# Two of twelve stores of gate blocks issued two chunks later in the ScalarE program of a PEER block kernel

## The chip, the cores and the metric

The kernel runs on one core of one Trainium2 chip. The metric is the device time of one execution in microseconds. The kernel before took 1569.04 us (median of 3 runs, 1568.71 to 1569.89).

## The reference

One transformer layer on 512 tokens of width 1024, in fp32: an adaptive RMS norm, a mixer with three kinds of attention heads, and then a PEER feed-forward, to which this change belongs. Cut to the feed-forward:

```
q = (x @ wq) as 8 heads x 2 halves x 128
s = q . sub_keys                     # 128 keys for each half
sv, si = top_k(s, 16)                # for both halves
top, pos = top_k(sv[0] + sv[1], 16)  # 16 experts of 16384 for each head
eidx = 128 * si[0][pos] + si[1][pos]
g = softmax(top)
a = gelu(u[eidx] . x)
y = sum(g * a * v[eidx])
```

A token uses 128 of 16384 experts. u and v are tables of 16384 rows of 1024.

## The kernel before, in words

The tokens are four tiles of 128. For the first tile (GT = 1) the rows of u and v of the chosen experts are gathered one by one, late in the kernel. The other three tiles (DT = 384 tokens) are computed densely: the experts are cut into 128 chunks of 128 (chunk i has the first key i in the order of `u_t`), each chunk's a = gelu(u x) is made for all 384 tokens, multiplied by a dense matrix of gates that is zero where an expert was not chosen, and then multiplied by v.

**A chunk of u.** SyncE loads 512 KB into one of two places of `u_raw` (`load_u`, L1080), once u_lo of the chunk two before has been made. ScalarE rounds it to `u_hi` (`u_high`, L1435; it also waits until TensorE is through with the chunk two before). VectorE subtracts to get `u_lo` (`split_u`, L2003). TensorE runs 24 matmuls of 128x128 by 384 columns (L857 to L859: hi by hi, hi by lo, lo by hi, for 8 parts of the width), into one of two PSUM banks. ScalarE takes the gelu of it into `a_act` (`gelu`, L1472) and, for the first 56 chunks, stores the 192 KB to `spill` in DRAM (`early_gelu`, L1484). In ScalarE's program `u_high(i + 2)` stands ahead of `early_gelu(i)`.

**The gates.** For each of the three dense tiles VectorE decodes the experts' two key numbers (`decode`, L2010 to L2025), TensorE turns them to columns (L872), and VectorE copies these to `cols` (L2051). Then, for 4 tokens at a time, VectorE makes one-hot rows `hot_i` and `hot_j` (L2058, L2060), TensorE multiplies them (L886), and ScalarE copies the result to `g_out` (L1506). A block is 32 tokens: eight such steps, 2 MB in `g_out`, which has two places. At the end of a block ScalarE waits for its own copies and issues the store of the block to `gates` in DRAM (L1512, L1513). There are 12 blocks, `tb` from 0 to 11, four in each tile.

**The order.** It is written out by hand. Beside each block run two chunks of u, chunk `beside(tb)` and the one after. Between the tiles come chunks without gates, `BETWEEN`: chunks 0 to 23 ahead of the first tile of gates, 32 to 35 between the first and the second, 44 to 51 between the second and the third, 60 to 63 behind the third. So block 3 (chunks 30 and 31) is followed by chunk 32 and block 7 (chunks 42 and 43) by chunk 44. VectorE's program has the decoding of the next tile among the chunks between, and `split_u` of the chunk that follows them (36 after the first tile) ahead of the copy to `cols`:

```
for n in rest + [BETWEEN[tile].stop]:
    split_u(n)
ps = taken(dve, ("cols", tile))
dve.tensor_copy(cols[:, :, tile * P:tile * P + P], ...)
```

TensorE's program has the transposes to columns in the middle of the last chunk between the tiles (35 and 51), and each gates matmul ahead of a quarter of a chunk.

The stores of the gates and of the gelus are issued on ScalarE's DMA queue, the loads of u on SyncE's. Both use the same 16 DMA engines. The semaphores `s_gst` count the gate stores of either place of `g_out`; ScalarE waits for them before it fills the place again, and SyncE and VectorE wait for all of them before the second half of the work begins.

Of the kernel before, what the change touches and what calls it, by code (L numbers as in the profile page):

```python
# [9 lines left out]
NT = S // P  # L10
# [8 lines left out]
GT = 1  # L19
DT = S - GT * P  # L20
GB = 32
# [76 lines left out]
def peer_block_kernel(nc, x, c_col, norm1_col, w_ada, b_ada, w_in, w_out, lam_vecs, subln_row, sinks_row,  # L98
# [4 lines left out]
    with ctx:  # L103
# [3 lines left out]
        def sem(name):  # L107
            return ctx.enter_context(nc.semaphore(name))
# [4 lines left out]
        def at(name, kib, shape, dt=f32):  # L113
            return nc.alloc_sbuf_tensor_at(name, shape, dt, offset=base + int(kib * 1024))
# [73 lines left out]
        g_out = [at("g_out0", 112, [P, P, GB]), at("g_out1", 140, [P, P, GB])]  # L188
# [102 lines left out]
        s_hot, s_gm, s_gt = sem("hot_rows_ready"), sem("gates_made"), sem("gates_taken")  # L291
        s_as, s_al = [sem("gelus_stored0"), sem("gelus_stored1")], [sem("gelus_loaded0"), sem("gelus_loaded1")]
        s_gst = [sem("gates_stored0"), sem("gates_stored1")]
        s_x2, s_f2, s_fm, s_fs, s_res = (sem(n) for n in ("x2_ready", "x2_squares", "x2_mean", "x2_std", "result_ready"))

        gates = nc.dram_tensor("gates", [DT // GB, P, NCHUNK, GB], f32).ap()
# [7 lines left out]
        def after(eng, s, n):  # L304

            if isinstance(n, int) and n < 1:
                return
            eng.wait_ge(s, n)

        def within(i, last=NCHUNK - 1):  # L310

            return not isinstance(i, int) or i <= last
# [47 lines left out]
        def over(i, c, n):  # L360

            return i // n if isinstance(i, int) else (i - c) // n + c // n
# [3 lines left out]
        BETWEEN = [range(0, 24), range(32, 36), range(44, 52), range(60, 64)]  # L366
# [7 lines left out]
        def beside(tb):  # L374

            return BETWEEN[tb // 4].stop + 2 * (tb % 4)
# [65 lines left out]
        for J, (i, j) in enumerate(JOBS):  # L442
            for qt, kk, _, _ in plan[j][1]:
                for n in (TILES.index(qt), TILES.index(kk)):
                    if n not in known:
                        NEEDS[J] = NEEDS.get(J, []) + [n]
                        known.add(n)
            v = {"C": 3, "A": 7, "B": 12}[plan[j][0]]
            if v not in known:
                VALUES[J] = [v]  # L450
                known.add(v)
# [4 lines left out]
        def _(pe):  # L456
# [170 lines left out]
            def pv(J):  # L627


                i, j = JOBS[J]  # L630
                kind, _, _, _, col, _, n, _ = plan[j]
                g = GROUP_OF[J]
                b = f"O{g % 2}"
                ps = take(b, ("o", g)) if J == FIRST[g] else bank[b]
                for v in VALUES.get(J, ()):
                    for t in range(NT):
                        emptied(("v", v, t))
                emptied(("pT", J))
                ahead = kind == "B" and n >= 4
                first = col if ahead else col - HD  # L640
                place = HD + n * HD if ahead else n * HD
                kt = key_tiles(i, j)
                for a, t in enumerate(kt):
                    mm = pe.matmul(ps[:, place:place + 2 * HD], pT[:, J % 2, a * P:a * P + P],  # L644
                                   v_sb[:, t, first:first + 2 * HD], start=(a == 0), stop=(a == len(kt) - 1))
                mm.then_inc(full[b] if J == LAST[g] else s_pv, 1)
# [297 lines left out]
            def both(m, c, late, _):  # L944
                if at_end(m):
                    if m == NCHUNK - TAIL:
                        last_v_chunks()
                    return
                v_chunk(m, c)
                if not late and not (isinstance(m, int) and m + NEXT >= NCHUNK):  # L950
                    a_chunk(m + NEXT, c + 1)
# [286 lines left out]
        def _(act):  # L1238
# [131 lines left out]
            for J in range(-1, N):  # L1370
# [14 lines left out]
                if J in LAST[0:4]:  # L1385
                    i = LAST.index(J)
# [42 lines left out]
            def u_high(i, c):  # L1429

                if not within(i):
                    return
                after(act, s_a, i - 1)
                act.wait_ge(s_u[c % 2], 16 * (over(i, c, 2) + 1))
                act.activation(u_hi[c % 2][:, :], u_raw[:, c % 2, :], ACT.Copy).then_inc(s_uhi, 1)  # L1435
# [18 lines left out]
            def v_high(i, c):  # L1454
                if not within(i):
                    return
                end = at_end(i)
                if end:
                    act.wait_ge(s_acc, PH * TOPK)
                else:  # L1460
                    after(act, s_yv, i - 1)
                act.wait_ge(s_v[c % 4], 16 * (over(i, c, 4) + 1))
                act.activation(v_hi_end[:, i % TAIL, :] if end else v_hi[:, c % 2, :], v_raw[c % 4][:, :], ACT.Copy)\  # L1463
                   .then_inc(s_vhi, 1)

            def gelu(i, slot, c):

                if not within(i):
                    return
                early = isinstance(i, int) and i < EARLY  # L1470
                act.wait_ge(s_a, i + 1)
                act.activation(a_act[:, bass.ds(slot, 1), :].rearrange("p o t -> p (o t)"),  # L1472
                               bank[f"S{c % 2}" if early else f"O{c % 2}"][:, 0:DT], ACT.Gelu).then_inc(s_gelu, 1)

            def early_gelu(i):

                if i >= SPILL:
                    act.wait_ge(s_as[i % 2], 16 * (SPILL // 2))
                    gelu(i, i % AHEAD, i)
                    return  # L1480
                after(act, s_as[i % 2], 16 * (i // 2))
                gelu(i, i % AHEAD, i)
                act.wait_ge(s_gelu, i + 1)
                act.dma_start(spill[i], a_act[:, i % AHEAD, :]).then_inc(s_as[i % 2], 16)  # L1484

            u_high(1, 1)
            for i in BETWEEN[0]:
                u_high(i + 2, i + 2)
# [3 lines left out]
                if NUMBERS_AT <= i < NUMBERS_AT + NT:  # L1492
                    t = i - NUMBERS_AT
# [6 lines left out]
            for tile in range(NT - GT):  # L1500
                for tb in range(4 * tile, 4 * tile + 4):
                    i = beside(tb)
                    after(act, s_gst[tb % 2], 16 * (tb // 2))
                    for b in range(GB // 4):
                        act.wait_ge(s_gm, tb * (GB // 4) + b + 1)
                        act.activation(g_out[tb % 2][:, :, 4 * b:4 * b + 4].rearrange("p i t -> p t i"),  # L1506
                                       bank[f"T{b % 2}"][:, :].rearrange("p (t i) -> p t i", t=4), ACT.Copy)\
                           .then_inc(s_gt, 1)
                        if b == 3:
                            u_high(i + 2, i + 2)  # L1510
                            early_gelu(i)
                    act.wait_ge(s_gt, (tb + 1) * (GB // 4))  # L1512
                    act.dma_start(gates[tb].rearrange("p i t -> p (i t)"),  # L1513
                                  g_out[tb % 2][:, :, :].rearrange("p i t -> p (i t)")).then_inc(s_gst[tb % 2], 16)
                    u_high(i + 3, i + 3)
                    early_gelu(i + 1)
                for i in BETWEEN[tile + 1]:
                    u_high(i + 2, i + 2)
                    early_gelu(i)
                    if i == EARLY - 2:  # L1520

                        act.wait_ge(s_gst[0], 16 * (BLOCKS // 2))
                        v_high(0, 0)
# [710 lines left out]
```

## Time and profile before

| | |
|---|---|
| median of 3 runs | 1569.04 us |
| the profiled execution's own time | 1569.89 us |
| its span, first to last instruction | 1568.1 us |
| TensorE busy | 1528.9 us, 98% |
| TensorE weight loads | 1364.6 us, 87% |
| VectorE busy | 1338.0 us, 85% |
| ScalarE busy | 660.4 us, 42% |
| GpSimd busy | 487.9 us, 31% |
| mean granted TensorE clock | 0.995 |
| moved by DMA | 398.77 MB, 254 GB/s on average |

In the rows PE is TensorE, DVE is VectorE, ACT is ScalarE, SP is SyncE; a q behind a name (ACTq, SPq) is a DMA issue on that engine. A time at the start of a line is us from the start of the span. In square brackets stands the idle time of the engine ahead of the instruction, and what ended it. Busy times of 98% are an average over the whole kernel; the change lies between 573 and 669 us.

### The profile page before, as it was taken

The numbers are of one execution on the slowest core, as the hardware profiler recorded it, in microseconds if no ns is written. First come the engines' busy times: TensorE is split into PE (matmuls) and PEld (weight loads), VectorE is DVE, ScalarE is ACT, GpSimd is POOL, SyncE is SP. The second block draws the span as 40 slices with busy tenths as digits, with TensorE's granted clock in tenths as the row PEclk, the third lists the DMA queues.
The fourth block names the chain that finished last, engine by engine and source line by source line (L and its number), as shares of the span: only waits on it lengthen the run. The fifth ranks groups of instructions, "written<-read, shape, count | busy, mean of one in ns | idle before, by whom it ended". The sixth has DMA issues, their size and how long they took to land.

```text
span 1568.1 us, 24587 instructions
## 1 busy us (share of the span) xinstructions
PE 1528.9 (98%) x8275; PEld 1364.6 (87%) x8275; DVE 1338.0 (85%) x2877; ACT 660.4 (42%) x1143; POOL 487.9 (31%) x450
## 2 busy tenths in 40 slices
PE   4999999999999999999999999999999999999997
PEld 4877767888999999999999999999999998888886
DVE  5688765649999989899698898899999998999977
ACT  3444563233344766647433333333333432333232
POOL 1121300033450000020265445456566663223000
PEclk9999999999999999999999999999999999999999
DMA  9744310132355565676799999999999999999773
GB/s 368 267 163 159 148 68 1 55 95 82 107 180 170 198 229 196 229 239 268 280 398 333 345 347 338 348 336 371 372 373 378 366 343 356 376 351 352 241 240 107
DMA packets 160468, 398.77 MB, mean 254 GB/s; under 512 B 11754, under 2 KB 75370, under 8 KB 158706
## 3 DMA queue, kind: packets, MB, share of 16 engines
q1 hardware_dynamic: 112992, 227.06, 41.7%
q0 software_dynamic: 36864, 134.23, 23.0%
q10 hardware_dynamic: 10514, 36.30, 5.9%
q8 instruction: 47, 0.77, 0.2%
q14 instruction: 51, 0.41, 0.1%
HBM read 359.27 MB, written 38.27 MB: 254 GB/s over the span
## 4 chain that ended last, share of the span: by engine, by line
PE 81%; DVE 14%; DMA 2%; ACT 2%; issue 1%; ACTq 0%; DVEq 0%; SPq 0%
PE bank_S L908 16%; PE bank_T L908 11%; PE bank_O L859 6%; PE bank_O L857 6%; PE bank_O L858 6%; PE bank_T L886 5%; PE bank_G L908 5%; PE bank_S L857 3%; PE bank_S L858 3%; PE bank_S L859 3%; PE bank_O L644 2%; DVE mod_acc L1910 1%; PE bank_S L611 1%; DVE v_sb L1903 1%; DVE v_sb L1916 1%
## 5 line engine op out<-in xcount | busy, mean ns | idle before, releaser
L1463 ACT ACTIVATE v_hi<-v_raw 128x1024 fp32r<-128x1024 f32 x124 | 131.7, 1062 | 332.5 <-PE bank_G L908 332.5
L1435 ACT ACTIVATE u_hi<-u_raw 128x1024 fp32r<-128x1024 f32 x128 | 135.9, 1061 | 244.8 <-PE bank_O L859 139.8
L1214 POOL COPY stage<-eidx 128x1 uint32<-128x1 uint32 (+1 forms) x128 | 75.5, 590 | 462.2 <-DVE eidx L2031 208.5
L857 PE MATMUL bank_S<-h_hi,u_hi 128*128 128x384 f32 x512 | 180.0, 352 | 0.7 <-DVE u_lo L2003 0.7
L1218 POOL DMA_INDIRECT row<-in_peer_u,stage x128 | 148.1, 1157 | 103.7 <-POOL stage L1214 103.7
L859 PE MATMUL bank_O<-h_hi,u_lo 128*128 128x384 f32 x512 | 171.9, 336 | 0.0
L857 PE MATMUL bank_O<-h_hi,u_hi 128*128 128x384 f32 x512 | 171.7, 335 | 0.0
L859 PE MATMUL bank_S<-h_hi,u_lo 128*128 128x384 f32 x512 | 171.6, 335 | 0.0
L858 PE MATMUL bank_S<-h_lo,u_hi 128*128 128x384 f32 x512 | 171.5, 335 | 0.0
L858 PE MATMUL bank_O<-h_lo,u_hi 128*128 128x384 f32 x512 | 171.5, 335 | 0.0
L2099 DVE SCALAR_TENSOR_TENSOR y<-row,wgt,y 128x1024 f32<-128x1024 f32 x128 | 166.0, 1297 | 0.0
L2109 DVE TENSOR_TENSOR v_lo<-v_raw,v_hi 128x1024 fp32r<-128x1024 f32 x124 | 152.0, 1226 | 12.3 <-ACT v_hi L1463 0.8
L2122 DVE SCALAR_TENSOR_TENSOR junk<-row,h 128x1024 f32<-128x1024 f32 x128 | 156.0, 1218 | 0.0
L1218 POOL DMA_INDIRECT row<-in_peer_v,stage x128 | 142.2, 1111 | 41.9 <-issue 30.3
L908 PE MATMUL bank_S<-v_hi,w_lo 128*128 128x512 f32 x372 | 125.4, 391 | 0.0
L908 PE MATMUL bank_S<-v_lo,w_hi 128*128 128x512 f32 x372 | 125.3, 391 | 0.0
L908 PE MATMUL bank_S<-v_hi,w_hi 128*128 128x512 f32 x372 | 125.3, 391 | 0.0
L1506 ACT ACTIVATE g_out<-bank_T 128x512 f32<-128x512 f32 x96 | 104.7, 1122 | 46.6 <-PE bank_T L886 38.2
L2058 DVE TENSOR_SCALAR hot_i<-iota_k,cols 128x128 f32<-128x128 f32 x384 | 107.2, 347 | 1.0 <-PE bank_T L886 0.2
L886 PE MATMUL bank_T<-hot_i,hot_j 128*128 128x128 f32 x768 | 101.8, 275 | 1.3 <-DVE hot_j L2060 1.3
L886 PEld LDWEIGHTS bank_T<-hot_i,hot_j 128*128 128x128 f32 x768 | 97.6, 191 | 3.8 <-issue 2.1
L857 PEld LDWEIGHTS bank_S<-h_hi,u_hi 128*128 128x128 f32 x512 | 96.5, 189 | 2.1 <-issue 1.9
(374 smaller groups left out, 3649.6 us busy)
## 6 DMA issues: line engine op xcount, KB each, us to landing
u_raw<-in_u_t SPq DMA_DIRECT2D x128, 512.0 KB, 4.9
v_raw<-in_peer_v SPq DMA_DIRECT2D x128, 512.0 KB, 6.8
gates<-g_out ACTq DMA_DIRECT2D x12, 2048.0 KB, 6.8
g_in<-gates SPq DMA_DIRECT2D x32, 768.0 KB, 10.5
ada_late<-in_w_ada SPq DMA_DIRECT2D x8, 2048.0 KB, 8.5
spill<-a_act ACTq DMA_DIRECT2D x56, 192.0 KB, 2.3
a_act<-spill SPq DMA_DIRECT2D x14, 768.0 KB, 10.3
w_raw<-in_w_in SPq DMA_DIRECT2D x20, 512.0 KB, 4.0
```

Of the source, the lines that this page charges most:

```text
L857: pe.matmul(ps[:, 0:DT], u_hi[q][:, kk], h_hi[:, GT:NT, k, :], start=(k == 0), stop=False)
L858: pe.matmul(ps[:, 0:DT], u_hi[q][:, kk], h_lo[:, GT:NT, k, :], start=False, stop=False)
L859: mm = pe.matmul(ps[:, 0:DT], u_lo[q][:, kk], h_hi[:, GT:NT, k, :], start=False, stop=(k == KD - 1))
L886: mm = pe.matmul(ps[:, tok * P:tok * P + P], hot_j[:, b % 2, tok, :], hot_i[:, b % 2, tok, :], start=True, stop=True)
L908: mm = pe.matmul(y_bank[t][half][:, :], w[:, q, tt], v[:, q, half * 512:half * 512 + 512], start=(first and n == 0), stop=False)
L1218: pool.indirect_dma_start(rows[slot][:, :], None, table[:, :], bass.IndirectOffsetOnAxis(stage[:, place:place + 1], 0))\
L1435: act.activation(u_hi[c % 2][:, :], u_raw[:, c % 2, :], ACT.Copy).then_inc(s_uhi, 1)
L1463: act.activation(v_hi_end[:, i % TAIL, :] if end else v_hi[:, c % 2, :], v_raw[c % 4][:, :], ACT.Copy)\
L2058: dve.tensor_scalar(hot_i[:, B % 2, tok, :], iota_k[:, :], cols[:, 0, n:n + 1], cols[:, 2, n:n + 1], ALU.is_equal, ALU.mult)
L2099: dve.scalar_tensor_tensor(out=y0[:, :], in0=rows[2 * place + 1][:, :], scalar=wgt[:, q], in1=y0[:, :], op0=ALU.mult, op1=ALU.add).then_in ...
L2109: dve.tensor_tensor(lo[:, q, :], v_raw[c % 4][:, :], hi[:, q, :].bitcast(f32), ALU.subtract)\
L2122: dve.scalar_tensor_tensor(out=junk[:, :], in0=rows[2 * place][:, :], scalar=1.0, in1=h2[:, 0, :], op0=ALU.mult, op1=ALU.mult, accum_out=d ...
```

## The change

The store of a block becomes a helper, `store_gates`. For the last block of the first and of the second dense tile (blocks 3 and 7) it is not issued at the end of the block, but after `u_high(i + 3)`, `early_gelu(i + 1)` and the `u_high` and `early_gelu` of the first chunk between the tiles. The other ten stores stay where they are.

```
+            def store_gates(tb):
+                act.wait_ge(s_gt, (tb + 1) * (GB // 4))
+                act.dma_start(gates[tb].rearrange("p i t -> p (i t)"),
+                              g_out[tb % 2][:, :, :].rearrange("p i t -> p (i t)")).then_inc(s_gst[tb % 2], 16)
...
-                    act.wait_ge(s_gt, (tb + 1) * (GB // 4))
-                    act.dma_start(gates[tb].rearrange("p i t -> p (i t)"),
-                                  g_out[tb % 2][:, :, :].rearrange("p i t -> p (i t)")).then_inc(s_gst[tb % 2], 16)
+
+                    wait = tb % 4 == 3 and tile < NT - GT - 1
+                    if not wait:
+                        store_gates(tb)
                     u_high(i + 3, i + 3)
                     early_gelu(i + 1)
                 for i in BETWEEN[tile + 1]:
                     u_high(i + 2, i + 2)
                     early_gelu(i)
+                    if wait and i == BETWEEN[tile + 1].start:
+                        store_gates(tb)
```

## Rows read from the trace of the kernel before

**Rows 1.** Busy time of each engine from 500 to 760 us, granted clock, DMA share, GB/s

```profile
500.00:760.00 260.00, 258.29 (x1756) 255.17 (x1755) 235.53 (x568) 161.69 (x177) 10.95 (x9) 1.00 0.63 227
```

**Rows 2.** Waits of TensorE, 500 to 760: us in total, times, longest us

```profile
PE bank_T L886 <- DVE hot_j L2060: 1.3, 3, 0.5
PE bank_S L857 <- DVE u_lo L2003: 0.4, 1, 0.4
```

**Rows 3.** Waits of ScalarE, 500 to 760

```profile
ACT u_hi L1435 <- DMA u_raw<-in_u_t: 15.9, 4, 4.7
```

**Rows 4.** Timeline of ScalarE, second tile's last store (start, us, what)

```profile
653.12 0.34 ACTq L1513 DMA_DIRECT2D gates<-g_out  x1
653.56 1.06 ACT L1435 ACTIVATE u_hi<-u_raw 128x1024 fp32r<-128x1024 f32 x1 [0.48 <-ACT g_out L1506]
...
658.60 0.33 ACTq L1484 DMA_DIRECT2D spill<-a_act  x1
663.26 1.06 ACT L1435 ACTIVATE u_hi<-u_raw 128x1024 fp32r<-128x1024 f32 x1 [4.69 <-DMA u_raw<-in_u_t]
```

**Rows 5.** Line L1513 from 653 to 654: us to landing

```profile
DMA to landing us min/median/max: 6.9/6.9/6.9
```

**Rows 6.** Chain that ended last, 560 to 700: two u_raw loads (start, us)

```profile
576.10 6.53 DMA u_raw<-in_u_t
...
655.98 7.19 DMA u_raw<-in_u_t
```

**Rows 7.** Line L1080 from 650 to 651 (one load, at 650.9)

```profile
DMA to landing us min/median/max: 3.6/3.6/3.6
```

**Rows 8.** Timeline of VectorE, second tile

```profile
664.42 1.23 DVE L2003 TENSOR_TENSOR u_lo<-u_raw,u_hi 128x1024 fp32r<-128x1024 f32 x1 [2.50 <-ACT u_hi L1435]
```

**Rows 9.** Timeline of TensorE, second tile, end of chunk 46 and start of 47

```profile
664.91 0.33 PE L858 MATMUL bank_S<-h_lo,u_hi 128*128 128x384 f32 x1
665.08 0.34 PE L859 MATMUL bank_S<-h_hi,u_lo 128*128 128x384 f32 x1
665.79 0.41 PE L857 MATMUL bank_S<-h_hi,u_hi 128*128 128x384 f32 x1 [0.38 <-DVE u_lo L2003]
```

**Rows 10.** Timeline of ScalarE, first tile's last store

```profile
573.23 0.34 ACTq L1513 DMA_DIRECT2D gates<-g_out  x1
...
578.71 0.33 ACTq L1484 DMA_DIRECT2D spill<-a_act  x1
582.71 1.06 ACT L1435 ACTIVATE u_hi<-u_raw 128x1024 fp32r<-128x1024 f32 x1 [4.03 <-DMA u_raw<-in_u_t]
```

**Rows 11.** Timeline of VectorE, first tile, u_lo of chunk 36

```profile
586.93 1.23 DVE L2003 TENSOR_TENSOR u_lo<-u_raw,u_hi 128x1024 fp32r<-128x1024 f32 x1
```

**Rows 12.** Timeline of TensorE, first gates matmul of the second and third tile

```profile
590.53 1.13 PE L886 MATMUL bank_T<-hot_i,hot_j 128*128 128x128 f32 x8 [0.48 <-DVE hot_j L2060]
...
687.61 1.13 PE L886 MATMUL bank_T<-hot_i,hot_j 128*128 128x128 f32 x8 [0.39 <-DVE hot_j L2060]
```

**Rows 13.** Line L1080, windows 579 to 581 and 659 to 660: when issued

```profile
L1080 SPq DMA_DIRECT2D u_raw<-in_u_t x1: 328/328/328, 579.7 to 579.7; - x1
...
L1080 SPq DMA_DIRECT2D u_raw<-in_u_t x1: 328/328/328, 659.5 to 659.5; - x1
```

**Rows 14.** DMA queues (q1 SyncE, q10 ScalarE): windows 654:659, 660:662.2, 659:660

```profile
q10 hardware_dynamic: 127, 2.08, 104.5%
q1 hardware_dynamic: 6, 0.01, 0.4%
...
q1 hardware_dynamic: 134, 0.50, 71.2%
...
q10 hardware_dynamic: 102, 0.13, 64.3%
```

**Rows 15.** Line L1513 from 573 to 574: us to landing

```profile
DMA to landing us min/median/max: 7.8/7.8/7.8
```

**Rows 16.** Tile g_out, all 12 gate stores: us to landing

```profile
DMA to landing us min/median/max: 6.5/6.8/8.4
```

## The prediction, made before the kernel was run

> **What bounds the kernel now.** I read the busy times by stretch first. From 500 to 760 us, the stretch in which the gates are made and stored, TensorE is busy for 258.29 of 260 us, at a granted clock of 1.00, so 2.4 GHz [rows 1]. Next I read whom TensorE waits for in that stretch: four waits, together 1.7 us, three for hot_j at the start of each tile's gates and one of 0.4 for a u_lo [rows 2]. Nothing else can be gained there. ScalarE does wait for loads of u_raw, 15.9 us in four waits [rows 3], but ScalarE is not the bound; such a wait costs only what reaches TensorE.
>
> The timeline shows where it does. In the second tile the last store of gates is issued at 653.12 and takes 6.9 us to land [rows 4, 5]. The u_raw load issued at 655.98 takes 7.19 us, where one with free DMA engines takes 3.6 [rows 6, 7]. Its u_hi starts at 663.26, u_lo at 664.42, and TensorE, whose matmuls follow one another each 0.17 us, starts the next chunk at 665.79 instead of one step after 665.08, at 665.26 [rows 4, 8, 9]: 0.53 us lost. In the first tile the same load, issued at 576.10, takes 6.53 us [rows 6]; u_hi comes at 582.71 [rows 10], and TensorE has no gap there. What follows in that tile is tight all the same: u_lo of chunk 36 (586.93), then the copy to cols, hot_i, hot_j, and the first gates matmul at 590.53 after a gap of 0.48 [rows 11, 12]. The third tile has 0.39 at the same place with no store before it [rows 12], so at most 0.09 us of that gap is the store's.
>
> **The change, part by part.** Everything here is reckoned on the profiled execution: 1569.89 us, of which the span is 1568.1. That execution is 0.85 above the median of 1569.04; differences are added to the median. A measurement of this kernel tells about 0.2%, 3.1 us, from no change.
>
> *Nothing is added in work.* Two stores of 2 MB, of 12, are issued later by ScalarE; the bytes, the instruction (0.34 us) and its wait stay. Where the wait stood, u_hi can start some 0.4 us earlier (653.56 less 653.12) [rows 4], but the u_hi behind it still waits for TensorE, so this is worth nothing. At the new place the wait for the gate copies is long fulfilled. The 0.34 us of issue lies in ScalarE's idle time before the next u_hi (4.69 us idle there before) [rows 4]. The buffer of the moved store is filled again two blocks later, behind eight copies, a store and two chunks of the other buffer; the moved store has landed long before, so no copy waits for it.
>
> *Gain.* The load of 655.98 no longer has the store in front. With 3.6 us, even with 5, it lands by 661.0, before TensorE frees its u_hi (a chunk of 4.16 us before 665.26, so 661.1). The gap of 0.53 us in the second tile goes. The 0.09 of the first tile I do not count, since the same buffer chain is late there for the next reason.
>
> *Cost.* The store is now issued right behind the spill store of the second chunk: about 0.4 after 578.71, so 579.1, and 0.4 after 658.60, so 659.0 [rows 4, 10]. Half a microsecond later SyncE issues the next u_raw loads, at 579.7 and 659.5 [rows 13]; these times are set by u_lo of the chunk two earlier, which does not move. Call L the time that these loads take.
>
> How late may they be? Second tile: chunk 47 starts at 665.26 with its gap gone, and 24 matmuls at 0.173 (a step of 0.17 in the rows) end at 669.42 [rows 9]. From start of u_hi to the first matmul is 665.79 - 663.26 = 2.53, from landing to u_hi 0.09 (655.98 + 7.19 = 663.17). So it must land by 666.8: L up to 7.3 is free. First tile: what counts is not TensorE's own need of chunk 36, which comes after the gates matmul, but VectorE's order. u_lo of chunk 36 stands ahead of the cols copy, and the copy ahead of hot_j. From u_lo to the gates matmul is 590.53 - 586.93 = 3.60; from u_hi to u_lo 1.16, landing to u_hi 0.09. Landing later than 590.53 - 4.85 = 585.7 delays TensorE one for one: L up to 6.0 is free. So:
>
> shift = (L - 6.0, not below 0) + (L - 7.3, not below 0) - 0.53.
>
> TensorE has no other wait in this stretch, so a shift at either place stays to the end.
>
> *L itself.* From 654 to 659 the ScalarE queue moved 127 packets, 2.08 MB, while the SyncE queue moved 6, though a load was issued at 655.98; that queue's 134 packets came at 660 to 662.2 [rows 14]. A load issued during the store is moved after it. So I take that one issued 0.5 us after it is as well. Before, the two loads landed 9.4 (576.10 + 6.53 - 573.2) and 10.05 us after their store's issue. Between stood a spill store, whose 102 packets kept the 16 engines 64% busy for 1 us, so 0.64 us [rows 14]; it now goes ahead of the store. This leaves 8.8 and 9.4, less the lag of 0.6 and 0.5: 8.2 and 8.9, mean 8.55. Those two stores took 7.8 and 6.9, mean 7.35, against a median of 6.8 over all 12 [rows 5, 15, 16]; with the median it would be 8.0. I take 8.3, between. Then the first tile costs 2.3, the second 1.0, less 0.53: **+2.8 us**, 1571.8. Bounds for L behind the store: below, 7.0 (the shortest store, 6.5, less the lag of 0.5, and the 1.6 us by which the first tile's load landed after its store, less the spill's 0.64); above, 9.5 (the second tile's 10.05 less 0.5, with the spill's 0.64 not gone). These give +0.5 and +5.2.
>
> The Trainium skill, "DMA: Bandwidth & Descriptors", section "Anatomy of one DMA — SWDGE (gpsimd) path", fits a transfer of GpSimd's path as 2.0 us plus its bytes by 436 GB/s: by it an estimate of 8.0 us for store and load as one, so L of 7.5 and a shift of +1.2. For the store alone it gives 6.8, which the trace agrees with; for the load alone 3.2, against 3.6 in the row.
>
> **Rivals.**
> *A. The whole tail comes on top (slower).* Place: the same two loads. If L is 8.5 or more, the shift is over 3.1 us; with 9.5 it is 3.5 + 2.2 - 0.5 = +5.2, 1574.2. For it speaks that one of the two loads seen landed 10.05 after the store's issue, and that the spill store of the next chunk and the next load queue up as well. Against it: ordinary stores take 6.5 to 6.8. The point of decision lies only 0.2 above the L that I take.
> *B. The queues share the engines (not slower).* The load is issued while the store has hardly begun, and its packets might get in between. With equal bytes each the load waits for as much of the store as it has itself, 0.5 of 2 MB, a quarter of 127 packets in 5 us: 3.6 + 1.25 = 4.9. L is below 6.0, nothing is late, and the shift is -0.5: 1568.5. For it speaks that store and load start together, which the trace does not show for 2 MB; against it, the 3 us in which a waiting load moved nothing.
> Here the Trainium skill, same page, section "Queues, rings and completion order", says that each DMA engine goes round between its queues, packet by packet. By that rule rival B would be nearer; the trace does not agree for the load of 655.98.
> That the change does not do what it says is ruled out by the code: the condition holds for blocks 3 and 7 and the loop issues each of them once, at chunks 32 and 44.
>
> **How the numbers follow.** Queued behind with L from 7.0 to 8.5: 0.52, time 1571.8. Rival A: 0.37, from 1572.2 to 1574.2. Rival B: 0.11, 1568.5. Under B the gain is far within 0.2%; I still leave 0.03 of its chance for faster, for what I don't see. So faster 0.03, same 0.52 + 0.08 = 0.60, slower 0.37. The range reaches from L = 7.0 less the spread of the median, 1568.9, to L = 9.5 with some 0.2 on top, 1574.4 (the runs of the kernel before lie within 0.9 of the median); what is outside is most of rival B and the end of A. The likeliest case's own range is 1569.5 to 1572.2.
>
> **What would show it.** In the trace after, the load near 655.6 to 656 takes 5 us or less, and the matmul gap near 665.3 is gone. The loads near 579.7 and 659.5 take 8 us or more, with ScalarE's u_hi waiting for them until about 588 and 668. TensorE waits near 590 for hot_j, 2.8 us instead of 0.5, and near 669.4 for u_lo, 1.0 us. If those loads take under 6 us the reckoning is wrong at L; if they take 8 and the gaps do not come, it is wrong at the order on VectorE. If the time moves by more than 5 us either way, something outside this stretch has moved.

## The result, and the profile after

The changed kernel takes 1574.14 us (median of 9 runs, 1573.13 to 1575.07), the kernel before in the same runs 1569.89 (9 runs, 1568.30 to 1570.62): 4.25 us slower, ratio 1.003 with an interval of 1.0022 to 1.0038. Run again on another occasion it took 1573.85 (median of 8 runs) against 1569.38, 4.47 us slower, ratio 1.0025 (1.0015 to 1.0036). That lies inside the range of the prediction, but on the side of its rival A: clear of noise, and slower by more than 0.2%.

The span grew from 1568.1 to 1572.4 us, and all of it in the stretch of the change. First the waits of TensorE from 500 to 765 us (us in total, times, longest), which answer to [rows 2]:

```profile
PE bank_T L886 <- DVE hot_j L2068: 3.5, 3, 2.7
PE bank_S L857 <- DVE u_lo L2011: 1.3, 1, 1.3
```

Before it was 1.3 and 0.4, so 3.1 us more of waiting. The timeline of TensorE has the two gaps, at the first gates matmul of the second tile [rows 12] and ahead of chunk 48:

```profile
592.35 1.13 PE L886 MATMUL bank_T<-hot_i,hot_j 128*128 128x128 f32 x8 [2.68 <-DVE hot_j L2068]
...
674.22 0.41 PE L857 MATMUL bank_S<-h_hi,u_hi 128*128 128x384 f32 x1 [1.26 <-DVE u_lo L2011]
```

Where they come from is on ScalarE's timeline, to be read beside [rows 4] and [rows 10]:

```profile
578.35 0.33 ACTq L1484 DMA_DIRECT2D spill<-a_act  x1
578.72 0.45 ACTq L1488 DMA_DIRECT2D gates<-g_out  x1
581.04 1.06 ACT L1435 ACTIVATE u_hi<-u_raw 128x1024 fp32r<-128x1024 f32 x1 [2.72 <-PE bank_S L859]
...
587.60 1.06 ACT L1435 ACTIVATE u_hi<-u_raw 128x1024 fp32r<-128x1024 f32 x1 [5.12 <-DMA u_raw<-in_u_t]
...
662.35 0.44 ACTq L1488 DMA_DIRECT2D gates<-g_out  x1
664.67 1.06 ACT L1435 ACTIVATE u_hi<-u_raw 128x1024 fp32r<-128x1024 f32 x1 [2.72 <-PE bank_S L859]
...
671.68 1.06 ACT L1435 ACTIVATE u_hi<-u_raw 128x1024 fp32r<-128x1024 f32 x1 [5.57 <-DMA u_raw<-in_u_t]
```

The chunk that waited for its load before (35 and 47) now waits for TensorE alone, at 581.04 and 664.67. The one behind it (36 and 48) waits for its load for over 5 us. The chain that ended last names both loads (start, us):

```profile
579.30 8.22 DMA u_raw<-in_u_t
...
662.93 8.67 DMA u_raw<-in_u_t
```

On VectorE the first of them holds up a queue of work, as the order in the code says (u_lo, cols, hot_i, hot_j):

```profile
588.77 1.22 DVE L2011 TENSOR_TENSOR u_lo<-u_raw,u_hi 128x1024 fp32r<-128x1024 f32 x1 [3.53 <-ACT u_hi L1435]
589.91 0.55 DVE L2059 COPY cols<-bank_G 128x384 f32<-128x384 f32 x1
590.49 1.11 DVE L2066 TENSOR_SCALAR hot_i<-iota_k,cols 128x128 f32<-128x128 f32 x4
591.52 0.68 DVE L2068 TENSOR_TENSOR hot_j<-iota_k,cols 128x512 f32<-128x512 f32 x1
```

The waits explain 3.1 of some 4.5 us. The rest is in no wait. It is in how long the matmuls take behind the first gap:

```profile
593.50 0.33 PE L858 MATMUL bank_S<-h_lo,u_hi 128*128 128x384 f32 x1
...
594.24 0.53 PE L858 MATMUL bank_S<-h_lo,u_hi 128*128 128x384 f32 x1
594.56 0.53 PE L859 MATMUL bank_S<-h_hi,u_lo 128*128 128x384 f32 x1
```

Their starts are 0.32 us apart instead of 0.17. The windows (stretch, its length, busy us and instructions of PE, PEld, DVE, ACT, POOL, then granted clock, DMA share, GB/s) show why:

```profile
592.30:593.70 1.40, 1.35 (x11) 1.38 (x12) 1.40 (x5) 0.12 (x1) 0.00 (x0) 1.00 0.87 336
593.70:597.10 3.40, 3.40 (x15) 3.40 (x14) 2.03 (x8) 1.25 (x2) 0.00 (x0) 0.50 0.01 4
597.10:600.50 3.40, 3.40 (x27) 3.40 (x26) 3.40 (x10) 1.96 (x2) 0.00 (x0) 0.99 0.00 0
```

For 3.4 us the granted clock is 0.50, 1.2 GHz, and TensorE gets through 15 matmuls instead of 27. The kernel before has 27 there at 1.00:

```profile
593.70:597.10 3.40, 3.40 (x27) 3.40 (x26) 3.40 (x9) 2.21 (x2) 0.00 (x0) 1.00 0.02 5
```

The engine is busy 3.40 of 3.40 us either way, so busy time does not show this loss. Before the clock fell, TensorE had waited 2.68 us, up to 592.35, and had then run for 1.35 us at 1.00.

So that the parts can be told apart, here are the starts of three instructions in each profiled execution: the transposes to columns at the end of the first stretch between tiles (A), the first gates matmul of the second tile (B), the transposes of the third tile (C).

| kernel | A | B | C | B - A | C - B | A to C against before |
|---|---|---|---|---|---|---|
| before | 587.47 | 590.53 | 684.62 | 3.06 | 94.09 | |
| changed | 587.09 | 592.35 | 688.86 | 5.26 | 96.51 | +4.62 |
| changed, again | 587.46 | 592.65 | 689.14 | 5.19 | 96.49 | +4.53 |
| block 3 alone | 587.38 | 592.64 | 686.07 | 5.26 | 93.43 | +1.54 |
| block 7 alone | 587.48 | 590.54 | 685.49 | 3.06 | 94.95 | +0.86 |
| u_lo behind hot rows | 587.52 | 590.57 | 686.50 | 3.05 | 95.93 | +1.83 |
| matmuls in the gap | 587.48 | 592.77 | 687.68 | 5.29 | 94.91 | +3.05 |
| block 3 alone, matmuls in the gap | 587.57 | 592.86 | 686.28 | 5.29 | 93.42 | +1.56 |
| store with the load | 586.26 | 591.02 | 686.85 | 4.76 | 95.83 | +3.44 |
| copy without a wait | 586.72 | 591.04 | 684.93 | 4.32 | 93.89 | +1.06 |
| store 1.1 us behind the load | 587.36 | 590.35 | 684.48 | 2.99 | 94.13 | -0.03 |
| two halves | 585.61 | 588.59 | 682.02 | 2.98 | 93.43 | -0.74 |

### The profile page after: what moved, and what is told of

Same layout as the page of the kernel before. It is cut to its first block, busy times and chain, and to the rows that moved or that the text cites. A ratio compares the mean times of both kernels' runs of the same rounds, so it can differ in the third digit from the quotient of the medians.

```text
span 1572.4 us, 24587 instructions
## 1 busy us (share of the span) xinstructions
PE 1529.5 (97%) x8275; PEld 1365.8 (87%) x8275; DVE 1337.3 (85%) x2877; ACT 659.6 (42%) x1143; POOL 485.3 (31%) x450
## 4 chain that ended last, share of the span: by engine, by line
PE 81%; DVE 14%; DMA 2%; ACT 1%; issue 1%; DVEq 0%; SPq 0%; ACTq 0%
PE bank_S L908 16%; PE bank_T L908 11%; PE bank_O L859 6%; PE bank_O L857 6%; PE bank_O L858 6%; PE bank_T L886 5%; PE bank_G L908 5%; PE bank_S L857 3%; PE bank_S L858 3%; PE bank_S L859 3%; PE bank_O L644 2%; DVE mod_acc L1918 1%; PE bank_S L611 1%; DVE v_sb L1911 1%; DVE v_sb L1924 1%
```

## The experiments

The theory after the result: (1) a load of u_raw issued half a microsecond behind a 2 MB store is moved after it and takes over 8 us; (2) in the first tile this reaches TensorE through VectorE's order, 2.2 us; (3) in the second, 1.4 us, less the gap removed; (4) TensorE's clock falls behind the longer gap, 1.4 us. The rivals stand with each run. Each difference is against the median of the kernel before in the same set of runs, and the ratio stands with its 95% interval.

**Block 3 alone.**

```
-                    wait = tb % 4 == 3 and tile < NT - GT - 1
+                    wait = tb == 3
```

> Only block 3 is stored two chunks on; block 7 is back at its old place. Theory (two late loads plus TensorE's clock): against the kernel before, +2.2 us for hot_j in the first tile, +1.4 us for the 3.4 us at half clock behind that gap, nothing in the second tile, where the gap of 0.5 at the end of chunk 46 stays: +3.6 us. Rival (the moved stores cost the same at both places, about half each): +2.1 us.

Measured: 1572.11 against 1569.40, +2.7 us (ratio 1.0016, 1.0007 to 1.0025). The gap is there in full:

```profile
592.64 1.13 PE L886 MATMUL bank_T<-hot_i,hot_j 128*128 128x128 f32 x8 [2.69 <-DVE hot_j L2068]
```

but the clock did not fall in this execution; the window of it reads

```profile
593.70:597.10 3.40, 3.40 (x26) 3.40 (x25) 3.40 (x11) 2.22 (x2) 0.00 (x0) 1.00 0.05 18
```

This was a miss in two ways. The first is the clock. The profiled execution, 1571.36 us, is the fastest of the 11, which go up to 1573.49, so it is not typical of them. Only the mean granted clock over the whole execution is on record for the others. A stretch of 3.4 us at half clock takes 0.001 from that mean (3.4 x 0.5 / 1570). It is 0.994 in 8 of the 11 and at least 0.995 in the three fastest, while 5 of the 33 executions of the kernel before beside them have 0.994 or less. So the clock most likely fell in most executions here; the measure is rough, since it also holds every other stretch at half clock. The second miss is C - B, 93.43, which is 0.66 below the kernel before with block 7 in its old place: the old gap of 0.53, most of that difference, is not in every execution either. The load behind that store took 6.5 us here, 7.19 in [rows 6].

**Block 7 alone.**

```
+                    wait = tb == 7
```

> Only block 7 is stored two chunks on. Theory: the load behind it takes 8.7 us, 1.4 more than is free, less the 0.53 gained at chunk 47: +0.9 us against the kernel before, with a gap of 1.3 us ahead of chunk 48 and the granted clock at 1.00 throughout. Rival (half of the loss each): +2.1 us.

Measured: 1570.80 against 1569.40, +1.4 us (ratio 1.0007, 0.9998 to 1.0016). The median and its interval could not tell 0.9 from 2.1, the trace does: +0.86 from A to C, the load 8.69 us, the gap 1.28, and the clock at 1.00.

```profile
659.55 8.69 DMA u_raw<-in_u_t
...
670.86 0.41 PE L857 MATMUL bank_S<-h_hi,u_hi 128*128 128x384 f32 x1 [1.28 <-DVE u_lo L2011]
```

**VectorE's order.** The change, with u_lo of chunk 36 made later:

```
-                for n in rest + [BETWEEN[tile].stop]:
+                for n in rest + ([BETWEEN[tile].stop] if tile != 1 else []):
                     split_u(n)
...
                                       ALU.is_equal).then_inc(s_hot, 1)
+                    if tile == 1 and B == tile * P // 4:
+                        split_u(BETWEEN[tile].stop)
```

> The changed kernel, but VectorE makes u_lo of chunk 36 behind the first hot rows of the second tile's gates instead of ahead of the copy to cols. Theory (VectorE's order carries the late load to TensorE): the load still takes 8.2 us, but the wait for hot_j falls from 2.7 to about 0.5 us, some 0.6 us return at the next two steps, and the clock stays at 1.00; the second tile's +0.9 stays: +1.4 us against the kernel before. Rival (chunk 36 itself is late on TensorE, or the loss lies elsewhere): +4.3 us as in the changed kernel.

Measured: 1571.05 against 1569.40, +1.65 us (ratio 1.0009, 0.9999 to 1.0018). ScalarE still waits 5.11 us for the load, but TensorE doesn't:

```profile
588.02 1.06 ACT L1435 ACTIVATE u_hi<-u_raw 128x1024 fp32r<-128x1024 f32 x1 [5.11 <-DMA u_raw<-in_u_t]
```

```profile
590.57 1.13 PE L886 MATMUL bank_T<-hot_i,hot_j 128*128 128x128 f32 x8 [0.47 <-DVE hot_j L2068]
593.34 1.13 PE L886 MATMUL bank_T<-hot_i,hot_j 128*128 128x128 f32 x8 [0.32 <-DVE hot_j L2068]
```

The gap at the first gates matmul is as short as in the kernel before, with a load just as late, and the clock stays at 1.00 (593.7 to 597.1). This shows (2): what was late for TensorE was not chunk 36 itself but the columns' copy behind its u_lo. The new order has a price of its own: the fifth gates matmul starts at 599.36, against 598.37 with block 7 alone. That is nearly all of the 0.98 us by which C - B is longer than there; 0.6 had been expected.

**Matmuls in the gap.** The change, and ahead of the second tile's gates:

```
+                if tile == 1:
+                    for n in range(14):
+                        pe.matmul(bank["S2"][:, 0:DT], h_hi[:, GT, n % KD, :], h_hi[:, GT:NT, n % KD, :],
+                                  start=True, stop=True)
```

> The changed kernel with 14 matmuls more (128x128 by 384 columns, 2.4 us) into the unused bank S2, ahead of the first gates matmul of the second tile; their results are not used. They fill the gap of 2.7 us. Theory (the clock falls because TensorE stood idle): the clock stays at 1.00 behind them and 1.4 us come back: +3.1 us against the kernel before, with the same 8.2 us for the load. Rival (the steps behind the gap are slow because VectorE and ScalarE come late, whatever TensorE does): +4.5 us as in the changed kernel, or more for the added matmuls.

> The changed kernel once more, unaltered, as the measure for the next one on the same chip. Both theories: +4.3 to +4.7 us against the kernel before. Theory on the clock: the granted clock falls to 0.50 for 3.4 us behind the gap of 2.7 us in most executions, perhaps not in all.

Measured: the changed kernel 1573.85 (8 runs) and this one 1574.70 (6 runs), against 1569.38: +5.3 us for this one (ratio 1.0033, 1.0021 to 1.0046), where +3.1 was expected. The median contradicts the expected gain, the trace does not. The added matmuls fill the gap but for 0.28 us, B - A is 5.29 as without them, and C - B falls from 96.49 to 94.91, 1.58 us, to the 94.95 of block 7 alone. In the changed kernel run again, the granted clock from 594.0 to 597.4 was 0.50. Here the rows are:

```profile
589.90 2.59 PE L881 MATMUL bank_S<-h_hi 128*128 128x384 f32 x14
```

```profile
593.70:597.10 3.40, 3.40 (x26) 3.40 (x26) 3.38 (x11) 2.24 (x2) 0.00 (x0) 1.00 0.13 42
```

What took part of it back lies elsewhere, behind the third tile's last store, which nothing had moved. That store took 9.6 us to land, 8.0 in the changed kernel. ScalarE waits 5.14 us for a load there, where the changed kernel waits 3.81, and TensorE has a gap:

```profile
763.80 1.06 ACT L1439 ACTIVATE u_hi<-u_raw 128x1024 fp32r<-128x1024 f32 x1 [5.14 <-DMA u_raw<-in_u_t]
```

```profile
766.27 0.41 PE L857 MATMUL bank_S<-h_hi,u_hi 128*128 128x384 f32 x1 [0.76 <-DVE u_lo L2015]
```

From C to the end of the span this execution takes 1.0 us more than the kernel before. With the 3.05 from A to C that is 4.1 us. The median is 0.57 above this execution, the fastest of the 6, so the trace accounts for most of the +5.3, not for all of it.

**The same with block 3 alone.**

> Only block 3 moved, with the 14 added matmuls in the gap. Theory on the clock: the gap of TensorE's own work stays 2.7 us long, the clock stays at 1.00 in every execution, so +2.2 us against the kernel before and no execution with the 1.4 more; with block 7 in its old place nothing else is lost. Rival (something behind the gap costs, which the added matmuls do not heal): +3 us or more, as when both blocks were moved and the matmuls added.

Measured: 1572.62 against 1569.18, +3.4 us (ratio 1.0020, 1.0011 to 1.0029), from 1571.85 to 1573.21; the clock is 1.00 behind the gap. Expected was +2.2. Again the load behind the third tile's last store is late (the store takes 9.8 us to land, ScalarE waits 5.31 us, TensorE has a gap of 0.9), and from C to the end this execution takes 1.2 us more than the kernel before. Why 14 matmuls 160 us earlier change a load there is open; no run tells it.

What the two runs say of (4): the first shows it by the segment from B to C, 1.58 us less with the clock at 1.00. The second cannot show it that way, since the profiled execution of block 3 alone had kept its clock too (93.42 and 93.43). The mean clocks of all executions point the same way: 0.994 or less in 17 of 28 executions without the added matmuls (the changed kernel twice, block 3 alone), in 1 of 17 with them. The totals do not show the gain; they are higher with the added matmuls in both cases.

**Store together with the load.** The change, with a wait ahead of the moved store for the count that SyncE waits for ahead of the load:

```
                     if wait and i == BETWEEN[tile + 1].start:
+                        act.wait_ge(s_ulo, i + 3)
                         store_gates(tb)
```

> The changed kernel, but ScalarE waits for u_lo of the chunk that frees the place of u_raw before it issues the store of blocks 3 and 7. SyncE waits for the same count to issue the load, so store and load go out together, the load ahead or beside it. Theory (a load is moved after a store issued ahead of it, not after one issued behind it): the two loads take 3.5 to 5 us instead of 8.2 and 8.7, the next ones, issued 4 us later, about 5; no gap at either place, -0.5 us against the kernel before. Rival (the queues share, and any 2 MB store near a load delays it): loads of 7 us or more, and +2 us or worse.

Measured: 1572.15 against 1569.40, +2.75 us (ratio 1.0018, 1.0009 to 1.0027). The theory failed here: issued within 0.01 us of each other, the load did not go ahead of the store.

```profile
578.48 7.71 DMA u_raw<-in_u_t
...
661.57 8.02 DMA u_raw<-in_u_t
```

The DMA queues tell how it went: this kernel from 579.5 to 584.5 (q10 ScalarE, q1 SyncE; packets, MB, share of 16 engines),

```profile
q10 hardware_dynamic: 96, 1.57, 73.3%
q1 hardware_dynamic: 109, 0.45, 25.6%
```

and the changed kernel from 579.9 to 584.4:

```profile
q10 hardware_dynamic: 96, 1.57, 93.9%
q1 hardware_dynamic: 16, 0.07, 3.5%
```

Issued together, the queues take turns, one piece of 4 KB for one of 16 KB, so the load ends about when the store does (8.3 us). Issued 0.6 us behind, it gets almost nothing until the store is through. Either way it takes about 8 us. Here the gap at B was 2.18 us, and the clock fell behind it:

```profile
592.30:595.70 3.40, 3.40 (x16) 3.40 (x15) 1.91 (x7) 1.12 (x2) 0.00 (x0) 0.50 0.02 7
```

**Store 1.1 us behind the load.** A first try put a copy between, but did not wait for its end:

```
+                        act.wait_ge(s_ulo, i + 3)
+                        act.activation(junk[:, :], x_sb[:, 0, :], ACT.Copy)
                         store_gates(tb)
```

> As the store behind the load, but ScalarE makes one copy of 1.06 us more (x_sb to a place not in use) between the wait for u_lo and the store, so that the store is issued 1.1 us behind the load of u_raw instead of together with it. Theory (what is issued first is moved first; issued together they take turns): the load takes 3.6 to 5 us, the next, issued some 3 us behind the store, 6.5 to 7.2, which is just free: gap of 0.5 at the first gates matmul, none at the chunks, -0.5 us against the kernel before. Rival (the engines are shared even so): the load takes 7 us or more, and the kernel +2.5 us or worse.

Measured: 1571.54 against 1569.38, +2.2 us (ratio 1.0015, 1.0006 to 1.0024). The loads take 7.27 and 7.5 us; the gap at B is 1.74 us, and the clock behind it stayed at 1.00. The store was not 1.1 us behind, as it was meant to be: it is the run above once more, because the DMA issue did not wait for the ACTIVATE ahead of it:

```profile
578.94 1.06 ACT L1528 ACTIVATE junk<-x_sb 128x1024 f32<-128x1024 f32 x1 [0.99 <-DVE u_lo L2013]
578.95 0.36 ACTq L1488 DMA_DIRECT2D gates<-g_out  x1
```

With a semaphore behind the copy the order holds:

```
+                        act.activation(junk[:, :], x_sb[:, 0, :], ACT.Copy).then_inc(s_pause, 1)
+                        act.wait_ge(s_pause, tile + 1)
```

> As the run before with the copy, but ScalarE now waits for the copy to be finished before it issues the store, which it had not: there the store went out in the same instant as the load. Now it is to stand 1.1 us behind the load of chunk 36 or 48. Theory (what is issued first is moved first): that load takes 3.6 to 5 us, the next one, 3 us behind the store, 6.5 to 7.2 (free up to 7.3): gap of 0.5 at the first gates matmul, none at the chunks, -0.5 us against the kernel before, 0 at worst. Rival (the engines are shared whatever the order): 7 us or more for the load, and +2 us.

Measured: 1569.79 against 1569.18, +0.6 us (ratio 1.0003, 0.9994 to 1.0012): the loss is gone within the noise, and from A to C the trace has -0.03 us. The rival, a load of 7 us or more whatever the order, fell.

```profile
579.58 1.07 ACT L1529 ACTIVATE junk<-x_sb 128x1024 f32<-128x1024 f32 x1 [0.99 <-DVE u_lo L2015]
580.68 0.34 ACTq L1489 DMA_DIRECT2D gates<-g_out  x1
...
585.48 1.06 ACT L1436 ACTIVATE u_hi<-u_raw 128x1024 fp32r<-128x1024 f32 x1 [2.72 <-PE bank_S L860]
```

u_hi of chunk 36 now waits for TensorE and not for its load. The load after it, issued 3.1 us behind the store in the second tile, is late instead (7.57 us, where 6.5 to 7.2 had been expected, and a gap of 0.2 at TensorE), so nothing is gained over the kernel before either.

**Two halves.**

```
-                    if wait and i == BETWEEN[tile + 1].start:
-                        store_gates(tb)
+                    if wait and i - BETWEEN[tile + 1].start in (0, 1):
+                        store_gates(tb, i - BETWEEN[tile + 1].start)
```

Each call stores 64 of the 128 keys of the block; the counts on `s_gst` are raised to match.

> The changed kernel, but the stores of blocks 3 and 7 are cut into two of 1 MB: the first half two chunks on, the second three chunks on. Theory (a load issued behind a store waits for the whole of it, some 5 us for 2 MB, so 2.5 for 1 MB): the loads behind either half take 5.7 us instead of 8.2 and 8.7, under the 6.0 and 7.3 that are free; no loss at either place, the granted clock at 1.00: -0.5 us against the kernel before. Rival (the loss comes with any store among the chunks between): +2 us or more.

Measured: 1569.61 against 1569.18, +0.4 us (ratio 1.0001, 0.9992 to 1.0010). TensorE has no gap at a chunk in the stretch: the loads behind the first halves don't hold up their u_hi at all, and the one behind the second half in the second tile lands 7.1 us after its issue at 661.8, just under the 7.3 that are free. The expected 5.7 us was too low there. A to C is 0.74 us shorter than before, the expected 0.5 and a little more, but the profiled execution, 1567.34 us, is the fastest of the 11. The medians do not resolve it: the best version found equals the kernel before and does not beat it.

**One chunk on.**

```
                     early_gelu(i + 1)
+                    if wait:
+                        store_gates(tb)
...
-                    if wait and i == BETWEEN[tile + 1].start:
-                        store_gates(tb)
```

> Both stores issued one chunk on instead of two. They then stand 0.5 us ahead of the loads of chunks 35 and 47. Theory (L = 8.3 us for a load issued that way, VectorE's order as before): in the first tile u_hi of 35 at 584.0, decoding done 0.8 us later than the columns want it, the first gates matmul 1.3 us late; in the second tile chunk 47 0.6 us later than before: +1.9 us against the kernel before. Rival (each chunk further on costs more, so half way costs half): +2.2 us or so, with a gap of 2 us or more at one place.

Measured: 1571.70 against 1569.38, +2.3 us (ratio 1.0013, 1.0004 to 1.0022); in the profiled execution +1.3, against an expected 1.9 (C at 686.38 instead of 684.62, with the first tile's columns at 507.80 instead of 507.38). The loads issued 0.6 us behind the stores take 8.13 and 8.17 us, and TensorE has gaps of 0.72 and 0.76 us at chunks and 0.54 at the gates. The L of such a load holds at a third place; the reckoned loss was 0.6 us too high. The rival's gap of 2 us did not come.

## Why the prediction was wrong

Right were, point by point:

- *The gain.* The loads of chunks 35 and 47 went out of the way, and the gap of 0.53 at chunk 47 is gone. The profiled execution of block 3 alone, with block 7 in its old place, shows that this gap was not always there.
- *L.* Taken as 8.3, measured 8.22 and 8.67. That the load is moved behind a store issued half a microsecond ahead was right: 16 of its packets against 96 of the store's in 4.5 us. One term was read short: the 102 packets of [rows 14] are counted up to 660, but the spill store goes on beside the load until 661, 160 packets in all, and in the changed kernel too a spill store runs beside the end of the load (144 packets from 586.5 to 588). So part of the good hit at L may be luck.
- *The free time.* 6.0 in the first tile and 7.3 in the second. With the measured L the formula gives 2.2 + 1.4 - 0.5 = 3.1; block 3 alone moved B by 2.20, block 7 alone made the second stretch 0.86 longer (1.37 - 0.53 = 0.84). Both halves of the sum hold to a tenth in these executions, and VectorE's order as the way was shown by the reordered run.
- *Rival B* fell: no load issued together with 2 MB or 0.6 us behind it took under 7.2 us. The queues do take turns, but only when both are issued together, and piece for piece, not byte for byte.

Wrong was one step of the sum: "+2.8 us" as the whole, with "a shift at either place stays to the end" as all that follows from a gap. The granted clock of 1.00 was read for the kernel before, whose longest gap in the stretch is 0.48 us, and carried over to a kernel for which the same text foresaw a gap of 2.8. Behind it the clock fell to 0.50 for 3.4 us, which costs 1.55 us (96.51 less 94.95 from B to C). The sum had this term at nothing, without a reason. 3.1 + 1.5 is 4.6; the segment A to C has 4.62 and the medians 4.25 and 4.47. That term moved the outcome from the boundary of 0.2% to clearly beyond it. Rival A named the right side for another reason: at an L of 8.5 and over. With the measured L, mean 8.45, the waits alone stay at the boundary, 3.1. That the measured time lies inside the range of the prediction is luck: its upper part was there for an L of up to 9.5, and no load took more than 8.7.

On this point the Trainium skill, "TensorE: Matmul & The Clock Gate", section "Part 1: The HAM clock gate", says that the array's clock is gated to half by how busy the engine was. The runs agree with it: 0.50 behind a wait of 2.68 us, 1.00 in both runs where matmuls filled an equally long wait for hot_j. One execution with a gap of 2.69 us kept 1.00 all the same.

The Trainium skill, "DMA: Bandwidth & Descriptors", section "Queues, rings and completion order", which the prediction cites, says that each DMA engine goes round between its queues, packet by packet. The trace agrees for transfers issued together (109 and 96 packets in 5 us), and does not for a load issued 0.6 us behind (16 and 96 in 4.5 us).

## What to carry to other kernels

Moving a large transfer off one load puts it ahead of the next; ask which load is issued next behind it, how late that one may land, and what stands behind its consumer in each engine's order. If a gap at TensorE of the size seen here (2.2 to 2.7 us) is foreseen, price the clock as well as the gap, and read the granted clock behind it rather than busy time. If a large store must lie among tight loads, try cutting it or issuing it a microsecond behind a load: here both brought the time back to that of the kernel before, and neither beat it. A DMA issue needs a semaphore if it is to stand behind an ACTIVATE. And look at more than the profiled execution: twice here it was the fastest of 11.

## What the runs showed of the hardware

- A 2 MB store of 16 KB pieces and a 512 KB load of 4 KB pieces, issued together on two queues: 109 load packets and 96 store packets in the same 5 us, the load 7.7 us. Issued 0.6 us behind: 16 load packets in 4.5 us, the load 8.2 us. With the load issued 1.1 us ahead of the store, its u_hi was not held up at all.
- The fall of the clock is not the same in every execution: behind a gap of 2.69 us it stayed at 1.00 in one profiled execution and fell in two of the changed kernel (2.68 and 2.61, to 0.50 in both); behind one of 2.18 it fell in another, behind 1.74 and less it stayed.
- Executions differ in the clock elsewhere too: from 34 to 44 us its mean is between 0.50 and 0.66 (0.52 in the kernel before) in 11 of the 13 profiled executions, and at 1.00 in those of block 3 alone and block 7 alone.
- A DMA issue on ScalarE's queue came 0.01 us after an ACTIVATE of 1.06 us ahead of it had begun.
- 14 matmuls added at 590 us came with a wait of ScalarE for a load at 760 us that was over 1 us longer, in both kernels that had them; the cause was not found.
